# Retention scores in head pairs, low weights last in token jobs, and the order of loads before chunk 10

## The reference, cut to what matters

```python
h = rmsnorm(x, norm1_g[l])
p = h @ w_in[l]
...
q = rotary(q.reshape(B, S, RET_HEADS, RET_QK_DIM), cos, sin)
k = rotary(k.reshape(B, S, RET_HEADS, RET_QK_DIM), cos, sin) * (RET_QK_DIM ** -0.5)
...
scores = jnp.einsum('bhnid,bhnjd->bhnij', qc, kc) * decay_in[:, None]
inner = jnp.einsum('bhnij,bhnje->bhnie', scores, vc)
...
y = y * lax.rsqrt(jnp.mean(y * y, axis=-1, keepdims=True) + EPS)
return (y.reshape(B, S, RET_V_WIDTH) * jax.nn.silu(g)).astype(p.dtype)
```

## Time and profile before

| | us |
|---|---|
| median of three runs | 2818.44 |
| lowest, highest run | 2814.32, 2818.74 |
| profiled execution | 2812.87 |
| its span, first to last instruction | 2811.1 |
| TensorE busy in it | 2757.9 |
| GpSimd, VectorE, ScalarE busy | 1400.6, 1286.0, 1101.2 |

### The profile page before, as it was taken

The page is one execution under the profiler, slowest core; times in us unless marked ns, Lnnn a source line. Parts: engine busy times, 40 slices in busy tenths (PEclk is TensorE's granted clock), DMA queues, the critical chain, the costliest instruction groups (busy, mean ns, idle before and its releaser), DMA issues. The chain is left out here.

```text
span 2811.1 us, 46630 instructions
## 1 busy us (share of the span) xinstructions
PE 2757.9 (98%) x18980; PEld 2057.5 (73%) x18981; DVE 1286.0 (46%) x1791; ACT 1101.2 (39%) x1618; POOL 1400.6 (50%) x1767
## 2 busy tenths in 40 slices
PE   8999999999999999999999999999999999999997
PEld 6777777888888877777788888877778764445543
DVE  6255433467751525543446775168855232222223
ACT  5485334343332448533434333355574321111112
POOL 6377446666665637744666665665655321111110
PEclk9999999999999999999999999999999999999999
DMA  5222122222232422212222223232222149999995
GB/s 182 74 87 73 48 106 91 85 92 104 90 113 98 163 76 86 73 48 104 91 86 91 105 90 113 93 113 81 92 91 94 56 195 408 414 420 413 411 409 233
DMA packets 63368, 413.98 MB, mean 147 GB/s; under 512 B 9792, under 2 KB 10560, under 8 KB 25920
## 3 DMA queue, kind: packets, MB, share of 16 engines
q1 hardware_dynamic: 63168, 411.18, 38.7%
HBM read 401.71 MB, written 4.19 MB: 144 GB/s over the span
## 5 line engine op out<-in xcount | busy, mean ns | idle before, releaser
L113 POOL TENSOR_TENSOR w_lo<-w,next_hi 128x256 fp32r<-128x256 f32 (+1 forms) x1272 | 1001.6, 819 | 622.9 <-ACT next_hi L1679 290.0
L1679 ACT CAST next_hi<-w 128x1024 fp32r<-128x1024 f32 (+1 forms) x152 | 156.9, 1032 | 462.4 <-PE bank L1497 443.0
L113 POOL TENSOR_TENSOR mid_w_lo<-w,mid_w_hi 128x256 fp32r<-128x256 f32 x240 | 199.0, 862 | 138.7 <-ACT mid_w_hi L2805 138.3
L3567 PE MATMUL bank<-moe_w,moe_hg 128*64 128x512 f32 x1024 | 225.8, 594 | 0.0
L3567 PEld LDWEIGHTS bank<-moe_w,moe_hg 128*64 128x64 f32 x1024 | 73.4, 137 | 141.1 <-issue 140.5
L3504 POOL COPY moe_quad_place<-moe_place 128x16 f32 (+1 forms) x7 | 1.4, 196 | 346.4 <-PE bank L3621 346.4
L1492 PE MATMUL bank<-h_hi,next_hi 128*128 128x512 f32 x688 | 170.8, 390 | 0.0
L1494 PE MATMUL bank<-h_lo,next_hi 128*128 128x512 f32 x688 | 169.9, 389 | 0.0
L1497 PE MATMUL bank<-h_hi,w_lo 128*128 128x512 f32 x688 | 169.9, 389 | 0.0
L1325 ACT CAST next_hi<-w 128x1024 fp32r<-128x1024 f32 x96 | 80.2, 835 | 206.6 <-PE bank L1523 151.6
L1492 PEld LDWEIGHTS bank<-h_hi,next_hi 128*128 128x128 f32 x688 | 129.2, 188 | 27.7 <-issue 1.0
(11 more groups left out here) (633 smaller groups left out, 6237.9 us busy)
## 6 DMA issues: line engine op xcount, KB each, us to landing
moe_w<-in_moe_w SPq DMA_DIRECT2D x128, 1024.0 KB, 13.2
moe_w<-in_moe_w SPq DMA_DIRECT2D x32, 2048.0 KB, 12.4
w<-in_ffn_up SPq DMA_DIRECT2D x44, 1024.0 KB, 4.8
w<-in_w_merge SPq DMA_DIRECT2D x48, 768.0 KB, 4.3
w<-in_w_in SPq DMA_DIRECT2D x30, 1024.0 KB, 4.8
w<-in_w_mid SPq DMA_DIRECT2D x29, 1024.0 KB, 4.8
w<-in_ffn_down SPq DMA_DIRECT2D x16, 1408.0 KB, 5.9
w<-in_w_out SPq DMA_DIRECT2D x16, 512.0 KB, 4.3
```

The costliest lines, as they stand in the source:

```text
L113: ins = nc.gpsimd.tensor_tensor(out[:, ks, :], raw[:, ks, :], high[:, ks, :].bitcast(F32), ALU.subtract)
L1679: nc.scalar.copy(split(B.w_hi, n), raw(n)).then_inc(f["w_hi"], 1)
L3567: mm = nc.tensor.matmul(bank[half_of(u), :], hg[:, k, slots_of(b, u)], w[:, u, k * 512:k * 512 + 512], start=(k == 0), stop=(k == KD - 1))
```

## The change

- **Scores**: `scores(pair, part)` makes the products of two heads of a pair next to each other, on the two halves of the rows, in two parts of two key tiles each, after jobs 8, 9 (pair 0) and 11, 13 (pair 1). The decayed scores of the two heads have homes of their own (`sc`). `decays` follows that order; for pair 1 it waits for the values of head 0 or 1.
- **Retention steps one job later**: values after jobs 10, 12, 14, 16, squares after 11, 13, 15, 17, and ScalarE's square and root likewise. VectorE's shifts of tiles 12 and 13 stand ahead of `head_out(2)`.
- **Loads**: chunk 10 is issued behind SyncE's wait for `ret_done` 4 and the three small loads, no longer ahead of them. VectorE waits for these loads behind `centre`, not ahead of `measure`.
- **Token jobs**: in the front phase two token tiles at a time take all high products, then low activations, then low weights, so 16 products come before the wait for the low weights, not 8. In the mid phase all four or two tiles do: 32 or 16 products. Job 4 waits for four early tiles, job 5 for eight.
- **Borders**: GpSimd makes the first half of the low part of tile 1, VectorE the second (`next_low_end`).

```diff
@@ -105,10 +105,10 @@
...
-def low_parts(nc, out, raw, high):
+def low_parts(nc, out, raw, high, pieces=LOW_PIECES):
     n = out.shape[1] // LOW_PIECES
-    for i in range(LOW_PIECES):
+    for i in range(pieces):
         ks = slice(i * n, (i + 1) * n if i < LOW_PIECES - 1 else out.shape[1])
...
@@ -125,7 +125,15 @@
...
     raw = T.w[:, 0, 0:KD * 256].rearrange("p (k c) -> p k c", k=KD)[:, :, t * P:t * P + P]
-    low_parts(nc, T.w_lo[:, t, :, :], raw, T.next_hi[:, t, :, :])
+    low_parts(nc, T.w_lo[:, t, :, :], raw, T.next_hi[:, t, :, :], LOW_PIECES // (t + 1))
+
+
+def next_low_end(nc, T, dve):
+
+    dve.wait_ge(T.sems["next"]["w_hi"], 2)
+    ks = slice(KD // 2, KD)
+    raw = T.w[:, 0, 0:KD * 256].rearrange("p (k c) -> p k c", k=KD)[:, ks, P:2 * P]
+    nc.vector.tensor_tensor(T.w_lo[:, 1, ks, :], raw, T.next_hi[:, 1, ks, :].bitcast(F32), ALU.subtract)
...
@@ -200,7 +208,19 @@
...
         self.cossin, self.ret_tmp = at(spare, 8, "cossin", 2, S), at(spare, 12, "ret_tmp", 2, S)
-        self.sc, self.rstd = at(spare, 16, "sc", 4, S), at(spare, 24, "rstd", S)
+        first, second = at(spare, 16, "sc_first", 5 * P * 2), at(spare, 8, "sc_second", 7 * P)
+        second_end, self.rstd = at(spare, 21, "sc_second_end", 3 * P), at(spare, 24, "rstd", S)
+        begin = (0, 4 * P, 7 * P, 9 * P)
+
+        def sc(u, jc):
+            n = S - jc * P
+            if u == 0:
+                return first[:, begin[jc]:begin[jc] + n]
+            if jc < 2:
+                return second[:, begin[jc]:begin[jc] + n]
+            return second_end[:, begin[jc] - begin[2]:begin[jc] - begin[2] + n]
+
+        self.sc = sc
         self.swapped = at(spare, 18, "swapped", 4, S)
...
@@ -217,6 +237,11 @@
...
 RW_FIRST, U_FIRST = 18, 30
+
+
+def score_number(pair, jc, u):
+
+    return 8 * pair + 2 * jc + u + 1
...
@@ -294,7 +319,7 @@
...
-                if c > 2:
+                if 2 < c < 10 or c > 10:
                     fetch(c)
...
@@ -309,6 +334,7 @@
...
                         [P, S])).then_inc(f["prep_loaded"], 16)
+                    fetch(c)
             sync.wait_ge(f["w_lo"], jobs - 2)
...
@@ -365,21 +391,24 @@
...
                 h_hi, h_lo = h_parts(n)
-                if n == Z_JOBS:
-                    pe.wait_ge(f["early_hi"], KD)
-                    pe.wait_ge(f["early_lo"], KD)
-                for m in range(4):
+                early = n in (Z_JOBS, Z_JOBS + 1)
+                if early:
+                    pe.wait_ge(f["early_hi"], half * (t + 1))
+                for m, lhs, w in ((m, lhs, w) for b in range(2) for lhs, w in ((h_hi, hi), (h_lo, hi), (h_hi, lo))
+                                  for m in (2 * b, 2 * b + 1)):
                     bank = T.ps[m // 2][:, (m % 2) * 256:(m % 2) * 256 + 256]
-                    if t == 0 and m % 2 == 0:
+                    opening, closing = lhs is h_hi and w is hi, w is lo
+                    if t == 0 and m % 2 == 0 and opening:
                         pe.wait_ge(f["took"][m // 2], c)
-                    for lhs, w in ((h_hi, hi), (h_lo, hi), (h_hi, lo)):
-                        if w is lo and m == 0:
-                            pe.wait_ge(f["w_lo"], n + 1)
-                        for k in range(half):
-                            mm = nc.tensor.matmul(bank, lhs(half * t + k)[:, m * P:m * P + P], w[:, k, :],
-                                                  start=t == 0 and m % 2 == 0 and k == 0 and lhs is h_hi and w is hi,
-                                                  stop=t == 1 and m % 2 == 1 and k == half - 1 and w is lo)
-                    if t == 1 and m == 1:
+                    if early and lhs is h_lo and m == 0:
+                        pe.wait_ge(f["early_lo"], half * (t + 1))
+                    if closing and m == 0:
+                        pe.wait_ge(f["w_lo"], n + 1)
+                    for k in range(half):
+                        mm = nc.tensor.matmul(bank, lhs(half * t + k)[:, m * P:m * P + P], w[:, k, :],
+                                              start=t == 0 and m % 2 == 0 and k == 0 and opening,
+                                              stop=t == 1 and m % 2 == 1 and k == half - 1 and closing)
+                    if t == 1 and m == 1 and closing:
                         mm.then_inc(f["half"], 1)
...
@@ -405,15 +434,16 @@
...
-            def scores(h):
-
-                q = slice(64 * (h % 2), 64 * (h % 2) + 64)
+            def scores(pair, part):
+
                 pe.wait_ge(f["rotated"], 4)
-                for jc in range(4):
-                    if h:
-                        pe.wait_ge(f["decayed"], 4 * (h - 1) + jc + 1)
-                    nc.tensor.matmul(T.ps[2 + jc][:, 0:S - jc * P], qk[q, 2 + h // 2, jc * P:jc * P + P],
-                                     qk[q, h // 2, jc * P:S], start=True, stop=True).then_inc(f["scored"], 1)
+                for jc in (2 * part, 2 * part + 1):
+                    if pair or part:
+                        pe.wait_ge(f["decayed"], score_number(pair, jc, 1) - 4)
+                    for u, q in enumerate(HEAD_HALVES):
+                        nc.tensor.matmul(T.ps[2 + 2 * (jc % 2) + u][:, 0:S - jc * P],
+                                         qk[q, 2 + pair, jc * P:jc * P + P], qk[q, pair, jc * P:S], start=True,
+                                         stop=True).then_inc(f["scored"], 1)
...
@@ -423,10 +453,9 @@
...
                 for jc in range(4):
-                    pe.wait_ge(f["decayed"], 4 * h + jc + 1)
-                    mm = nc.tensor.matmul(T.ps[6][:, jc * P:S], vt[:, jc, h * P:h * P + P],
-                                          B.sc[:, jc, 0:S - jc * P], start=(jc == 0), stop=(jc == 3),
-                                          skip_group_check=True)
+                    pe.wait_ge(f["decayed"], score_number(h // 2, jc, h % 2))
+                    mm = nc.tensor.matmul(T.ps[6][:, jc * P:S], vt[:, jc, h * P:h * P + P], B.sc(h % 2, jc),
+                                          start=(jc == 0), stop=(jc == 3), skip_group_check=True)
                 mm.then_inc(f["summed"], 1)
...
@@ -485,12 +514,14 @@
...
                     feature_job(n)
+                if n in (11, 13, 15, 17):
+                    squares((n - 11) // 2)
+                if n in (8, 9):
+                    scores(0, n - 8)
+                if n in (11, 13):
+                    scores(1, (n - 11) // 2)
                 if n in (10, 12, 14, 16):
-                    squares((n - 10) // 2)
-                if n in (8, 10, 12, 14):
-                    scores((n - 8) // 2)
-                if n in (9, 11, 13, 15):
-                    values((n - 9) // 2)
+                    values((n - 10) // 2)
                 if n in (19, 20, 21, 22):
...
@@ -656,10 +687,10 @@
...
                     keep_high_h((2 * n - 8, 2 * n - 7))
-                if n in (9, 11, 13, 15):
-                    square((n - 9) // 2)
                 if n in (10, 12, 14, 16):
-                    root((n - 10) // 2)
+                    square((n - 10) // 2)
+                if n in (11, 13, 15, 17):
+                    root((n - 11) // 2)
                 if n == 17:
...
@@ -691,15 +722,16 @@
...
-            def decays(h):
-
-                if h:
-                    dve.wait_ge(f["summed"], h)
-                for jc in range(4):
-                    dve.wait_ge(f["scored"], 4 * h + jc + 1)
+            def decays(pair, part):
+
+                for jc in (2 * part, 2 * part + 1):
                     n = S - jc * P
-                    nc.vector.tensor_tensor(B.sc[:, jc, 0:n], T.ps[2 + jc][:, 0:n], B.decay[:, h, 0:n],
-                                            ALU.mult).then_inc(f["decayed"], 1)
+                    for u in range(2):
+                        if pair:
+                            dve.wait_ge(f["summed"], u + 1)
+                        dve.wait_ge(f["scored"], score_number(pair, jc, u))
+                        nc.vector.tensor_tensor(B.sc(u, jc), T.ps[2 + 2 * (jc % 2) + u][:, 0:n],
+                                                B.decay[:, 2 * pair + u, 0:n], ALU.mult).then_inc(f["decayed"], 1)
...
@@ -852,19 +884,23 @@
...
                 rotate(t)
-            for h in range(RET_HEADS):
-                decays(h)
-                if h == 3:
-                    shift(12, 12, B.sg_tmp[:, 0, :])
-                    shift(13, 13, B.sg_tmp[:, 1, :])
-                head_out(h)
+            decays(0, 0)
+            decays(0, 1)
+            head_out(0)
+            decays(1, 0)
+            decays(1, 1)
+            head_out(1)
+            shift(12, 12, B.sg_tmp[:, 0, :])
+            shift(13, 13, B.sg_tmp[:, 1, :])
+            head_out(2)
+            head_out(3)
             dve.wait_ge(f["ret_done"], RET_HEADS)
             link(nc.vector.memset(R.runs[:, :, :, 0:1], 1.0))
-            dve.wait_ge(f["prep_loaded"], 48)
             for m in range(4):
...
                 centre(m)
+            dve.wait_ge(f["prep_loaded"], 48)
             scan(0)
...
```

(21 more changed lines are left out.)

## The result

Slower, by about the smallest amount that can be told. The changed kernel took 2821.99 us (median of 13 runs, 2818.51 to 2824.09) against 2816.51 us (2812.22 to 2822.02, 13 runs): ratio 1.002, 95% interval 1.0012 to 1.0027, or +5.5 us. The forecast was 2814.9. The profiled execution took 2823.83 us (span 2821.8 us) where that of before took 2812.87 (2811.1): that one is at the fast end of its runs, so of the 10.7 us between the spans only about half is the change. From the front's first product to its fourth pair of products for decay and rate the changed kernel takes 156.05 us in layer 0 where before took 153.71, and 161.75 in layer 1 for 154.23: 2.3 and 7.5 us more.

The account below looks back on a forecast made before the run. TensorE, busy 98% of the 2811.1 us span, was taken as the bound. Terms -2.5 - 2.7 - 4.1 + 5.8 = -3.5 us against the median of 2818.44 gave 2814.9 us; own range 2809 to 2821, wide range 2803 to 2823.

Parts of the forecast that it names:

- part 5: Retention steps one job later, chunk 10 issued behind wait and small loads: 2.9 us slower net per layer, 5.8 both.
- part 4: Mid-phase token jobs with low weights last: more products cover the waits for GpSimd, 4.1 us gained.
- Part 1: Retention scores of two heads in pairs: 2.55 us a pair instead of 4.70, 4.3 us less per layer.
- Part 2: Borders, VectorE taking half of the second tile's low part: 1.4, 0.45 and 0.65 us gained, sum 2.5 us.
- Part 3: Front token job needing four early low tiles, not eight: 1.7 us gained in layer 0, 0.96 in layer 1, sum 2.7.
- The chunk lands much later: Rival: chunk 10 takes 12.4 us to land instead of 5.5, 6.9 us more per layer, 2828.7 us; chance 0.08.
- The clock fell: Rival: clock falls in the new stalls, showing only behind the third decay pair, 1.7 us per layer, 2818.3; chance 0.14.

Follow-up runs that it names:

- run 9: Run 3's kernel, with the load that the decay products read signalling on a semaphore of its own: 2800.79 us, ratio 0.9945.
- run 10: Run 9's kernel, with layer 1's residual store issued behind chunk 5 instead of chunk 2: 2798.33 us, ratio 0.994.
- run 3: The changed kernel with chunk 10 requested ahead of the heads wait and the mid-phase Sigmoids behind the bank 1 copy: 2805.07 us, ratio 0.9963.
- run 4: The changed kernel, with chunk 11 requested only when chunk 10 has landed: 2822.26 us, ratio 1.0026.
- run 7: The changed kernel without its retention part (borders and both new token-job orders alone): 2810.63 us, ratio 0.9977.
- run 8: The kernel before the change, with the two mid-phase Sigmoids behind the copy that empties bank 1: 2817.36 us, ratio 1.0002.
- run 2: The changed kernel, with the two mid-phase Sigmoids behind the copy that empties bank 1: 2818.85 us, ratio 1.0009.
- run 5: The changed kernel, with chunk 10 issued ahead of the three small loads, still behind the wait for the heads: 2813.88 us, ratio 0.9989.
- run 6: The kernel before the change with the retention part alone (paired scores, later steps, late chunk 10): 2827.62 us, ratio 1.0041.
- run 1: The changed kernel, with chunk 10 requested ahead of the wait for the finished heads again: 2807.46 us, ratio 0.9972.
- run 11: The changed kernel, with 13 idle products of 512 columns issued ahead of job 20: 2828.66 us, ratio 1.0036.

## Why the prediction was wrong

The sign was wrong: -3.5 us forecast, +5.5 measured. 2821.99 lies just above the forecast's own range (2809 to 2821) and inside the wide one (2803 to 2823). The loss stands at the bound of 0.2% itself. Two steps failed, one in part 5 and one in part 4.

- **Part 1 was right.** Parts of the pair take 1.70 and 0.86 us, 2.56 for 2.55 forecast, and run 9 measures 4.2 us in layer 0 for 4.3.
- **Part 2 was right at two borders and too large at the first.** TensorE's gaps at the three borders were 1.97, 0.79 and 1.23 us and are 0.33, 0.32 and 0.54. At the second and third that makes 1.2 us for the 1.1 forecast. At the first the products ahead of the gap ran 1.0 us later, and the front begins at 20.39 for 21.05, only 0.7 us earlier. The gap there is 0.3 to 1.5 us in the ten kernels with this part (mean 0.9) and 1.5 to 2.0 in the three without it (mean 1.8), so it is worth about 0.9 us and not 1.4.
- **Part 3 was half right.** The waits of 1.7 us went in both layers. In layer 1 I took the order of products as what decides, 8 more of them before the low part. There the arrival of chunk 3 decides, while the DMA engines are full (shares of 1.0, run 10), and behind ScalarE's wait for it stands the copy that empties job 6's bank. What TensorE gained before was waited for in job 6: 1.7 to 3.6 us in most of the kernels with all parts, and the clock fell behind it in some. Layer 1's start (first product to the squares of head 3) takes 4.2 us more than layer 0's in the changed kernel, before 0.5, and in run 10, without the store ahead of chunk 3, nothing. So the loads are the cause. The wait's size varies (2.10 us in the changed kernel, 3.6 in run 3, 0.5 in run 4, 0.2 in run 7), and what decides it is open; the 3.7 us that neither half has alone (run 7) are here.
- **Part 4 gave nothing or a loss**, where 4.1 us of gain were forecast: "With four tiles 32 products come before the wait instead of 8, 2.9 us more cover: the wait of 2.1 us goes." It costs no product, but it needs all four tiles' banks at once. From the eight one-column products ahead of job 6 to the first attention products behind it (1890.53 to 1919.09) the kernel takes 28.6 us where before took 25.3, +3.3; up to the routing phase 1.9 come back, which is what I forecast for the memory values: 1.4 us lost. Against the two other traces with the old order, whose clock fell (26.7 us, run 8), it is +1.9 and -1.9, nothing. I had read which semaphore TensorE waited for, and not what it would wait for next: bank 1 came free 5.33 us behind the job's start in both kernels, and before, the product that needed it stood there, to 0.05 us. Runs 2 and 8 show both limits.
- **Part 5 had the right sign and half the size**, +5.8 for +11.9. The step that failed is "Between 4.8 and 3.9 - 0.5 + 4.8 = 8.2 us I take 5.5, near the lower end, as transfers overlap but for their data". They hardly do: the chunk let ScalarE start 7.8 and 9.2 us behind its issue, above my upper end in layer 1, and 4.9 us when it was issued ahead of the small loads (run 5), while a chunk less behind it changed 0.2 and 0.5 us (run 4). From the split on the chain was 1.1 us shorter than forecast (17.7 for 18.8): with 16.2 and 17.7 for 14.0 the third pair comes to 33.9 and 35.4 as measured, 3.7 us over the forecast in all. That is also nearly all of what the trace of run 6 has over the forecast (9.2 for 5.8); the rest of its +11.9 is within its interval. A second cost was in no part: the wait for the bias load, 5.1 us. In the changed kernel it lies mostly ahead of a longer wait, job 20's, and is swallowed; it shows once chunk 10 is early (runs 1, 3 and 9). With the 3.9 us that I had in hand there would be no such wait in layer 0; the bias took 5.7 and 7.2, and 5.8 in run 1, each time with a full chunk issued right behind it, which in the kernel before came 3.4 us later. No run tests that alone.
- **The rivals.** "The chunk lands much later" came nearest: landing over the forecast, by 2.3 and 3.7 us instead of 6.9. The clock fell, and not where I had priced it, behind the third of the stalls. Of job 20 I had said that a fall is swallowed, which run 11 bears out for the fall itself; the one behind job 6's wait in the mid phase is paid (1896.88: eight products in 2.08 us, 1.2 at the full clock).

The Trainium skill, "DMA: Bandwidth & Descriptors", Specifications, gives some 358 GB/s as a core's share of the memory and 435 GB/s as the ceiling of the fabric. The stretches here move 407 and 418 GB/s at a DMA share of 0.98 and 1.00: by the upper figure they are nearly full, and the lower one doesn't bound them. At 407 GB/s the 768 KB of the three small loads take 1.9 us by themselves. Had I put that on the chunk's own 4.8 us, and not 0.7, the landing would have been 6.7 us; measured are 7.6 and 7.8, and 9.2 in layer 1. The small loads did not go at that rate (0.78 of share and 255 GB/s in run 4 while they were under way); why is open.

## What to carry to other kernels

When a wait is to be removed, look up when everything else that the next products need comes free, not only the thing waited for: a new order of work pulls needs forward, and a limit just behind the first one is invisible in the list of waits. When a load is moved behind others, price it by the bytes that stand ahead of it, look at what comes right behind it too, and keep the load that the critical chain wants in front of the small ones; a semaphore shared by several loads makes the first wait for the last. The change's idea was good: with chunk 10 back in its place it is worth 0.3% (run 1), and 0.5 to 0.6% with the limits behind it moved too (runs 9 and 10).

## What was not expected of the hardware

Two waits of 2.14 and 2.15 us at the same place, with the same work before and after them, had different effects on the granted clock: 0.63 of full in the four microseconds behind one, 1.00 behind the other (run 8). And the same was seen at the bias load: 1.96 us in run 1 was followed by products at half speed (eight in 3.23 us), 1.92 us in run 3 was not. Whether a wait of some 2 us costs its length or 1.4 to 1.6 us more can't be forecast from its length here. Behind the 3.04 us of run 5 it was 2.8 us more (9.49 us from the first pair to the second, where run 3 takes 6.73).
